# A decoder trunk's conditioning product: units of half the rows by 512 columns, and a setup in two stages of four feature tiles

## What is computed

```python
cond = jax.nn.silu(c)                       # 1024 values
for l in range(DEPTH):                      # 2 layers
    mod = cond @ w_ada[l] + b_ada[l]        # w_ada[l]: 1024 x 6144
    sh1, sc1, g1, sh2, sc2, g2 = [m[:, None, :] for m in jnp.split(mod, 6, axis=-1)]
    h = _rms_norm(x, norm1_gain[l]) * (1.0 + sc1) + sh1
    proj = h @ w_in[l]
    ...                                     # four groups of attention heads
    x = x + g1 * (o @ w_out[l])
    h = _rms_norm(x, norm2_gain[l]) * (1.0 + sc2) + sh2
    x = x + g2 * _conv_glu_ffn(h, w_ffn_up[l], ffn_conv_w[l], ffn_conv_b[l], w_ffn_down[l])
return _rms_norm(x, final_gain)
```

## Time and profile before

| | us |
|---|---|
| median of 3 runs | 746.04 (745.95 to 746.46) |
| the profiled execution's own time | 746.99 |
| its span, first to last instruction | 745.3 |
| TensorE busy, matmuls | 719.6 (97%) |
| DVE busy | 502.6 (67%) |
| ACT busy | 394.8 (53%) |
| GpSimd busy | 125.9 (17%) |
| DMA, all 16 engines | 158.35 MB, 212 GB/s in the mean |

### The profile page before, as it was taken

One profiled execution on the slowest core, in us unless ns is written; L12 is line 12 of the kernel. 1 busy time (PEld: TensorE's weight loads), 2 busy tenths in 40 slices (PEclk: granted clock), 3 DMA queues, 4 the chain that ended last, 5 costly groups with the idle time before them and its releaser, 6 DMA issues.

```text
span 745.3 us, 14854 instructions
## 1 busy us (share of the span) xinstructions
PE 719.6 (97%) x6177; PEld 677.0 (91%) x6177; DVE 502.6 (67%) x894; ACT 394.8 (53%) x632; POOL 125.9 (17%) x91
## 2 busy tenths in 40 slices
PE   5879999999999999999999999999999999999997
PEld 4579888999999999999998988999999999999996
DVE  2364788645589797887756468974569666666674
ACT  2347754534575565656445765554457445544543
POOL 2000102204006455555110010130400000000001
PEclk9799999999999999999998999999999999999998
DMA  9999998728277768686944696383826555555501
GB/s 284 349 294 203 351 330 278 247 86 281 87 245 259 257 207 278 217 266 221 329 129 128 219 290 226 115 282 103 283 69 226 170 174 193 197 171 172 190 34 58
DMA packets 139830, 158.35 MB, mean 212 GB/s; under 512 B 4963, under 2 KB 133108, under 8 KB 139764
## 3 DMA queue, kind: packets, MB, share of 16 engines
q1 hardware_dynamic: 139764, 157.41, 66.3%
HBM read 155.76 MB, written 1.64 MB: 211 GB/s over the span
## 4 chain that ended last, share of the span: by engine, by line
PE 84%; ACT 5%; DVE 4%; issue 3%; SPq 2%; DMA 1%; POOL 0%; DVEq 0%; POOLq 0%; ACTq 0%
PE bank L896 23%; PE bank L897 23%; PE bank L898 23%; PE bank L910 5%; ACT w_hi L1316 2%; PE bank L1219 1%; DVE w_lo L1561 1%; PE bank L950 1%; PE bank L926 1%; ACT work L1472 1%; PE bank L1234 1%; PE bank L1235 1%; DMA direct<-in_w_ada 1%; PE bank L1112 1%; PE bank L1110 1%
## 5 line engine op out<-in xcount | busy, mean ns | idle before, releaser
L896 PE MATMUL bank<-act_hi,w_hi 128*128 128x256 f32 (+1 forms) x1040 | 298.2, 287 | 5.1 <-DVE act_lo L1576 4.4
L1561 DVE TENSOR_TENSOR w_lo<-raw,w_hi 128x2048 fp32r<-128x2048 f32 (+1 forms) x97 | 232.4, 2395 | 97.7 <-ACT w_hi L1316 97.6
L897 PE MATMUL bank<-act_lo,w_hi 128*128 128x256 f32 (+1 forms) x1040 | 294.3, 283 | 0.0
L898 PE MATMUL bank<-act_hi,w_lo 128*128 128x256 f32 (+1 forms) x1040 | 294.3, 283 | 0.0
L1316 ACT ACTIVATE w_hi<-raw 128x2048 fp32r<-128x2048 f32 (+1 forms) x97 | 183.0, 1888 | 146.6 <-PE bank L898 145.9
L896 PEld LDWEIGHTS bank<-act_hi,w_hi 128*128 128x128 f32 (+1 forms) x1040 | 198.7, 191 | 15.6 <-issue 14.3
L897 PEld LDWEIGHTS bank<-act_lo,w_hi 128*128 128x128 f32 (+1 forms) x1040 | 198.8, 191 | 0.1
L898 PEld LDWEIGHTS bank<-act_hi,w_lo 128*128 128x128 f32 (+1 forms) x1040 | 198.7, 191 | 0.0
L896 PE MATMUL bank<-mlp_hi,w_hi 128*128 128x256 f32 x352 | 99.9, 284 | 0.0
L898 PE MATMUL bank<-mlp_hi,w_lo 128*128 128x256 f32 x352 | 99.6, 283 | 0.0
L897 PE MATMUL bank<-mlp_lo,w_hi 128*128 128x256 f32 x352 | 99.6, 283 | 0.0
(11 more groups left out here) (194 smaller groups left out, 858.7 us busy)
## 6 DMA issues: line engine op xcount, KB each, us to landing
direct<-in_w_ada SPq DMA_DIRECT2D x48, 1024.0 KB, 9.2
raw<-in_w_ffn_up SPq DMA_DIRECT2D x44, 1024.0 KB, 5.2
raw<-in_w_in SPq DMA_DIRECT2D x22, 1024.0 KB, 6.4
raw<-in_w_ffn_down SPq DMA_DIRECT2D x22, 1024.0 KB, 5.1
raw<-in_w_out SPq DMA_DIRECT2D x8, 1024.0 KB, 5.4
bias<-toeplitz SPq DMA_DIRECT2D x4, 384.0 KB, 11.6
heads_out<-in_x SPq DMA_DIRECT2D x1, 1024.0 KB, 5.3
out<-heads_out SPq DMA_DIRECT2D x4, 256.0 KB, 2.4
```

The lines of the kernel that those rows point to most:

```text
L896: pe.matmul(dst, lh, rh, start=first, stop=False, skip_group_check=check)
L897: pe.matmul(dst, lh, rl, start=False, stop=False, skip_group_check=check)
L898: return pe.matmul(dst, ll, rh, start=False, stop=last, skip_group_check=check)
L1561: nc.vector.tensor_tensor(w_lo[n % RAW][:, s], raw[n % RAW][:, s], w_hi[n % RAW][:, s].bitcast(F32), ALU.subtract).then_inc(lo_done, 1)
```

## The change

**What it does.** For all pairs that TensorE multiplies, a unit is now half of the rows (four row tiles) of all 512 columns of the pair: its first unit has row tiles 0 to 3, its second 4 to 7. A load takes rows of 2 KB instead of 1 KB; `ada_half` makes four matmuls of 512 columns instead of eight of 256, and the sums of a bank open in the first unit and close in the second. The eight units that GpSimd sums are loaded as before.

With that a pair is 512 adjoining columns, and the setup is in two stages of four feature tiles: pairs 0 and 2 give shift and scale of tiles 0 to 3, pairs 4 and 6 those of tiles 4 to 7 (`SETUP_COLUMNS`). TensorE multiplies tiles 0 to 3 of the first two input units in one piece, and tiles 4 to 7 as schedule entries. Units 2 and 4 of the conditioning loads go out earlier in SyncE's queue: the second before the bias rows, the third before the two input units, the fourth before the bias table.

```diff
+SETUP_COLUMNS = (0, SETUP_ADA // 2, 2, SETUP_ADA // 2 + 2)
 def pair_units(l, u):
-    return (u // 2, u // 2 + SETUP_ADA // 2) if l == 0 and u < SETUP_ADA else (u, u + 1)
+    u = SETUP_COLUMNS[u // 2] if l == 0 and u < SETUP_ADA else u
+    return (u, u + 1)
...
-        s += [("unit", 0, 6, KT), ("evac", 0), ("split_hi", 3), ("unit", 1, 6, KT), ("evac", 1), ("split_lo", 3),
+        s += [("unit", 0, 4, KT), ("evac", 0), ("split_hi", 3), ("unit", 1, 4, KT), ("evac", 1), ("split_lo", 3),
...
-                if kind == "ada":
+                if kind == "ada" and (l, u) not in sum_no:
+                    half, c0 = u % 2, (u - u % 2) * UC
+                    sp.dma_start(slot[:, :].rearrange("p (k n) -> p k n", k=KT // 2),
+                                 w_ada[l].rearrange("(k p) n -> p k n", p=P)[:, 4 * half:4 * half + 4, c0:c0 + 2 * UC]).then_inc(
+                        direct_in[a % DSLOTS], 16)
+                elif kind == "ada":
...
             load_direct(0)
+            load_direct(1)
             rows(0, V_BADA, b_ada, 48)
...
-            load_direct(1)
+            load_direct(2)
             load_unit(0, 0)
             load_unit(0, 1)
+            load_direct(3)
             sp.dma_start(tab[0:BUCKETS, :], t5_table).then_inc(table_in, 16)
...
-            for a in range(2, SETUP_ADA):
+            for a in range(4, SETUP_ADA):
                 load_direct(a)
...
-                w = direct[a % DSLOTS][:, :].rearrange("p (k n) -> p k n", k=KT)
-                for i in range(2):
-                    for g in range(4):
-                        k = 4 * i + g
-                        mm = pe.matmul(pair_bank(l, u)[32 * g:32 * g + 32, half * UC:(half + 1) * UC], cond[:, k, :],
-                                       w[:, k, :], start=(i == 0), stop=(i == 1))
+                w = direct[a % DSLOTS][:, :].rearrange("p (k n) -> p k n", k=KT // 2)
+                for g in range(4):
+                    mm = pe.matmul(pair_bank(l, u)[32 * g:32 * g + 32, :], cond[:, 4 * half + g, :], w[:, g, :],
+                                   start=(half == 0), stop=(half == 1), skip_group_check=True)
                 mm.then_inc(direct_used, 1)
```

On ACT the two weight splits now come before the second pair's rows are taken, and four tiles are modulated in one piece, ahead of the copies of `diag` and of the conv rows; the last four follow the front half of `w_hi[2]`. On DVE `first_mod` is gone:

```diff
-            first_mod(0)
+            take_mod(0, 0)
             for i in range(2):
                 split_lo(i, unit_width(i))
-            for k in range(1, KT // 2):
-                first_mod(k)
+            take_mod(0, 2)
+            first_modulated(0)
+            take_mod(0, 4)
+            take_mod(0, 6)
+            first_modulated(1)
```

More of the change, by code:

```diff
@@ L1067, in _ @@
             ada_turn(0, 0)
-            ada_half(0, 2, 0, 0)
+            ada(0, 2)
             pe.wait_ge(table_in, 16 * 2)
@@ L1071, in _ @@
             pe.matmul(bank[4][0:3 * HEADS, 0:384], tab[:, :], buck[:, :], start=True, stop=True).then_inc(diag_up, 1)
+            ada_turn(0, 2)
             pe.wait_ge(rows_sem[1], 16 * 4)
@@ L1076, in _ @@
             mm.then_inc(vec_turned, 1)
[L1077 to L1085, removed]
+            first_units(0, 4)
+            ada(0, 4)
             ada_turn(0, 4)
[L1087 to L1090, removed]
+            ada(0, 6)
             ada_turn(0, 6)
@@ L1361, in _ @@
                 "p (l r) -> p l r", l=DEPTH)[:, :, 0:VROWS[0]], ACT.Copy).then_inc(vec_in, 1)
-            modulated(0, 0, 0, 0, 2)
             for i in range(2):
                 split_hi(i, unit_width(i))
+            take_rows(0, 2)
+            modulated(0, 0, 0, 0, 4)
             act.wait_ge(diag_up, 1)
@@ L1371, in _ @@
                     nc.scalar.activation(vec[:, l, P * t:P * t + n], bank[3][:, c0:c0 + n], ACT.Copy).then_inc(vec_in, 1)
-            take_rows(0, 2)
-            modulated(0, 0, 0, 2, 4)
             take_rows(0, 4)
-            modulated(0, 0, 0, 4, 6)
             take_rows(0, 6)
@@ L1379, in _ @@
             nc.scalar.activation(w_hi[2][:, front], raw[2][:, front], ACT.Copy).then_inc(front_hi, 1)
-            modulated(0, 0, 0, 6, KT)
+            modulated(0, 0, 0, 4, KT)
             nc.scalar.activation(w_hi[2][:, back], raw[2][:, back], ACT.Copy).then_inc(hi_done, 1)
@@ L1600, in take_mod @@
                 dve.wait_ge(ada_turned, n)
-                s = slice(2 * u, 2 * u + 4)
+                c0 = 2 * pair_units(l, u)[0]
+                s = slice(c0, c0 + 4)
                 nc.vector.tensor_reduce(mod[:, l, s], pair_bank(l, u)[:, :].rearrange("p (c g r) -> p c g r", g=4, r=32)[:, :, :, 0],
@@ L1604, in take_mod, with first_modulated @@
                 dve.wait_ge(mod_ready, n)
-                nc.vector.tensor_tensor(mod[:, l, s], mod[:, l, s], vec[:, l, V_BADA + 2 * u:V_BADA + 2 * u + 4],
+                nc.vector.tensor_tensor(mod[:, l, s], mod[:, l, s], vec[:, l, V_BADA + c0:V_BADA + c0 + 4],
                                         ALU.add).then_inc(mod_done, 1)
[L1608 to L1621, removed]
+            def first_modulated(c):
+                wait_mod(4 * c + 4)
+                own(nc.vector.scalar_tensor_tensor(amp[:, 0, 4 * c:4 * c + 4], mod[:, 0, KT + 4 * c:KT + 4 * c + 4], 1.0,
+                                                   vec[:, 0, V_N1 + 4 * c:V_N1 + 4 * c + 4], ALU.add, ALU.mult))
+                modulated(0, 0, 0, 4 * c, 4 * c + 4)
             def take_columns(l, u, n):
```

## The result

The changed kernel takes 750.03 us (median of 7, 747.91 to 751.02) against 746.04 (745.53 to 746.84): ratio 1.0046, interval 1.0036 to 1.0055. It is slower, and above the top of the range, 749.2. A second series of six executions later in the study gave 748.71 against 746.24, ratio 1.0026 (1.0014 to 1.0038): slower again, but by 2.5 us and not by 4.0, and inside the range. One execution of the whole study, the eighth of the repeated kernel before, took 1764.38 us and is left out of every figure. The profiled execution took 751.02, 4.0 above the one of before.

A forecast was written before the change was run, and what follows sets the result against it. TensorE is busy from 46 to 700 us, so the change acts in the first 46, on waits for transfers and a loop. Profiled 746.99 + 1.5 (setup) - 3.1 (half-clock stretch) = 745.4, median 744.4; range 741.8 to 749.2.

The forecast's parts named there:

- The transfers: Setup loads of w_ada: 2 KB rows run at 380 GB/s, 2.76 us a transfer instead of 3.01.
- The first four units: Setup's first conditioning units: the fourth transfer lands at 22.8 us and tile 0 starts at 29.3.
- Tiles 0 to 3: First input units in one piece: done at 35.0, ends 33.6 and 37.0, clock back to full at 32.
- The second stage, all at full clock: Setup after tile 3: 8.9 us to tile 4, 14.7 in all, complete at 49.7, +1.5 us.
- rival 2: Clock falls in the second stage's gap ahead of tile 4: about 1.4 us lost, 748.9 in all; chance 0.18.
- The 32 later units: Conditioning units behind the setup, two rounds of 512 columns for four of 256: taken as 0, at best 2.2 us less.
- A stretch at half clock far behind: Half clock from 388.97 to 395.80 us: a shift of about 1.5 us removes it, -3.1 us, six in ten.
- signs of being wrong: w_ada wait beyond 24 or below 22; completion off by over 2 us; half clock at 389, 184 or 537.

The follow-up runs named there:

- experiment 4: Changed kernel with 29 extra unused matmuls in the idle times of the setup's second stage: 747.66 us, ratio 1.0019 to the kernel before.
- experiment 1: Kernel before with the new unit format for the 16 later pairs behind the setup alone: 745.28 us, ratio 0.9989.
- experiment 3: Changed kernel with tiles 1, 2 and 3 of the first input units moved between the second stage's conditioning units: 745.99 us, ratio 1.0004 to the kernel before.

## Why the prediction was wrong

Point by point:

- *The transfers.* Right. 2 KB rows run at 383 GB/s; 380 was worked out between 348 and 398. The Trainium skill ("DMA: Bandwidth & Descriptors", Specifications) gives about 358 GB/s as the limit of HBM for a core, worked out as a stack's bandwidth over its two cores. Here one core runs alone, and the 383 GB/s measured are above that figure; the measurement decides.
- *The first four units.* Right: 22.4 and 29.2 for 22.8 and 29.3.
- *Tiles 0 to 3.* 35.8 for 35.0, within the ends (36.2 in the second profile): the clock stayed at half to 34.16. It had been taken to come back at 32, by the one stretch of before; that length too differs between two profiles of the kernel before (10.2 and 13.7).
- *The second stage, all at full clock.* The first half was right: 8.9 us forecast from tile 3 to tile 4, 9.1 measured. The second was not: 5.8 us forecast at full clock from tile 4 to completion; 5.44 with fillings (experiment 4), but 7.26 and 6.02 in the changed kernel, since the clock fell in the gap. This is rival 2, whose mechanism was stated with a price of 1.4 us (measured 0.6 and 1.8) and a chance of 0.18. It should have been the forecast. What stood against it, that a gap of 2.47 us had not made the clock fall before, was one draw: behind the same gap it fell in the second profile. The setup as a whole, sized at +1.5, measured +4.0 and +2.8.
- *The 32 later units.* Right: nothing lost (experiment 1), perhaps a little won.
- *"A stretch at half clock far behind ... A shift of about 1.5 us moves it. I take it that the stretch goes (-3.1)."* **This is the step that failed.** It was sized at -3.1, and from the end of the setup to 736 us the first profile shows 0.0 (a lag of 3.98 us at completion, 4.02 at 736.24). The stretch at 389 was in fact gone in the changed kernel, but two others stood in its place; and it was gone in the kernel before, unchanged, in its second profile, with one in its place. None of thirteen traces is without such a stretch. Where among the three stages the clock falls differs between executions of one program, in two out of two programs profiled twice. (The record does not say on which chip the first profiles were taken, so that a part of the chip in this is not excluded; but the mean granted clock of the changed kernel's seven first executions, one series, goes from 0.976 to 0.984.) It is no property of the program that a shift could remove, and it should have entered as scatter about the median, for both kernels alike, not as a term. A single profiled execution shows one draw of it. The close times of before, which the text counted for a fixed place, are no sign of one: the two profiles differ by 0.6 us, with falls in other places.

On the profiled executions the miss is 5.6 us (751.02 for 745.4): 3.1 in that term and 2.5 in the setup. Without the term the forecast was 747.5; with rival 2's 1.4 in it, 748.9, against 748.7 and 750.0 measured. The sign came out wrong from the term at 389 alone. That the second median falls so near 748.9 is partly luck, since each execution draws its falls. Two of the text's own signs of being wrong came: completion off by more than 2 us (in the first profile, 52.2 for 49.7; 51.4 in the second) and half clock in the stages at 184 and 537. The change lost because the tiles that used to be TensorE's work between a pair's steps were put ahead of them in one piece. That uncovered ACT's copies (0.77 twice), left the last loop as uncovered as before (2.48 against 2.47), with an idle time of 1.45 ahead of tile 0 in place of one of 1.48, and in the last gap the clock fell. Put back between the steps, they take all of it back, by the medians (experiment 3). How the loss divides between idle time and clock is known for single executions only: of 4.0 and 2.8 us at completion 1.1 and 0.9 are idle time.

## What to carry to other kernels

When dense work is collected into one piece, look for the waits that it used to cover, and price them twice: as idle time and as the clock that may fall behind them. Before a half-clock stretch in a profile becomes a term of a sum, profile the same program again; if it has moved, it is scatter. Unused matmuls in waits that can't be avoided can be worth it, but here they won 0.3% only where the wait for the transfer and the later gaps were all filled; in the wait for the transfer alone they won nothing that the medians show. And they must last until the transfer lands.

## What the runs showed of the hardware

- The clock fell where TensorE had not been idle. In the first profile of the changed kernel what ran ahead of the falls at 191.17 and 542.74 were one-column products and conditioning units, without a gap and at full clock:

```profile
187.50:191.17 3.67, 3.67 (x34) 2.63 (x36) 0.76 (x3) 0.83 (x2) 0.31 (x1) 1.00 1.05 357
539.30:542.74 3.44, 3.44 (x34) 2.57 (x36) 0.58 (x3) 0.83 (x2) 0.29 (x1) 1.00 1.04 358
```

- The Trainium skill ("TensorE: Matmul & The Clock Gate", Why this matters for your kernels) names idle gaps between bursts of matmuls as what lowers the clock in mid-kernel. The first trace of before agrees at 20.33, within 3.99 us without work, and near tile 4, where filling the gap of 2.48 us kept the clock up; the falls of the mean-square stages stand beside that rule.
- The edges of the clock's stretches lie at other times in each profiled execution of one program. In two profiles of the kernel before, the clock was at half from 13.51 to 16.92 and 20.33 to 30.57 in one, from 15.87 to 29.53 in the other.
- Rows of 2 KB from HBM gave 383 GB/s (24.40 to 34.00 of the changed kernel), 1 KB 348, and 4 KB 398.
- A unit of four matmuls of 512 columns holds TensorE as long as one of eight of 256: 1.92 us for two (35.80 in the timeline above) against 1.93.
